# Two output projections of a fused two-block kernel: 256-column products replaced by 512-column products

## The reference

```python
# first block
mixed = jnp.concatenate([o_sb.astype(x.dtype), o_gla], axis=-1) @ w_out[l]
x = x + (1 + gate1[:, None, :]) * mixed
h2 = modulate(rms_norm(x, g_norm2[l]), shift2, scale2)
u = causal_depthwise_conv(h2 @ w_up[l], w_conv[l], b_conv[l])
...
# second block
mix = jnp.concatenate([out_a, out_b], axis=-1) @ w_o[l] + b_o[l]
x = layer_norm(DN_ALPHA * x + mix, ln1_g[l], ln1_b[l])
ca = memory_cross_attention(x, mem, xa_wq[l], ...)
```

## Time and profile before

| | |
|---|---|
| median of three runs | 3327.65 us |
| the profiled execution: its own time | 3335.15 us |
| the profiled execution: its span | 3333.4 us, mean granted clock 0.937 |
| PE busy | 2944.9 us, 88% |
| DVE, ACT, POOL busy | 55%, 31%, 27% |
| out1: first transpose to last early product | 620 to 746 us |
| out2: the same | 2212 to 2335 us |

### The profile page before, as it was taken

How to read it: one execution, slowest core, us unless ns; L and a number is a source line. 1 busy time by engine, 2 the same in 40 slices (tenths; PEclk the granted TensorE clock), 3 DMA queues, 4 the chain that set the end, 5 groups by cost and what they waited for, 6 DMA issues and landing times. The chain is left out here.

```text
span 3333.4 us, 40635 instructions
## 1 busy us (share of the span) xinstructions
PE 2944.9 (88%) x15957; PEld 2528.6 (76%) x15957; DVE 1846.0 (55%) x2924; ACT 1028.8 (31%) x1466; POOL 903.5 (27%) x303
## 2 busy tenths in 40 slices
PE   4969998799999999979577377989999899999996
PEld 3869997688888888868466376779779688888885
DVE  7626775655555454571689676865335533333336
ACT  5414444232221222231556254643221211111111
POOL 1212331112333233240223321221121233333333
PEclk9989998799999999989788678999999999999998
DMA  6732233401101111201323232130101111111111
GB/s 225 269 92 71 71 75 127 162 19 65 51 38 63 38 50 38 76 13 62 97 70 111 60 83 61 43 122 26 57 20 70 64 38 50 50 50 50 50 50 51
DMA packets 112339, 240.06 MB, mean 72 GB/s; under 512 B 53524, under 2 KB 72471, under 8 KB 99015
## 3 DMA queue, kind: packets, MB, share of 16 engines
q1 hardware_dynamic: 107175, 220.70, 20.3%
q10 hardware_dynamic: 4320, 14.29, 1.3%
q0 software_dynamic: 704, 3.15, 0.3%
HBM read 202.58 MB, written 38.67 MB: 72 GB/s over the span
## 5 line engine op out<-in xcount | busy, mean ns | idle before, releaser
L1019 PE MATMUL psum<-h_hi,w_hl 128*128 128x512 f32 x2432 | 751.9, 390 | 16.8 <-DVE ffn_relu L1596 12.8
L1008 POOL TENSOR_TENSOR w_hl<-w_raw,w_hl 128x2048 fp32r<-128x2048 f32 x65 | 323.9, 4983 | 863.5 <-ACT w_hl L1002 863.5
L1019 PEld LDWEIGHTS psum<-h_hi,w_hl 128*128 128x128 f32 x2432 | 457.0, 188 | 113.8 <-issue 18.3
L1036 PE MATMUL psum<-w_hl,ffn_a_hi 128*128 128x512 f32 x1600 | 494.3, 390 | 6.5 <-DVE residual L1359 6.5
L1019 PE MATMUL psum<-h_lo,w_hl 128*128 128x512 f32 x1216 | 474.1, 390 | 0.0
L449 PE MATMUL psum<-w_hl,h_hi 128*128 128x256 f32 (+1 forms) x1920 | 355.8, 288 | 28.4 <-POOL w_hl L412 13.9
L1036 PEld LDWEIGHTS psum<-w_hl,ffn_a_hi 128*128 128x128 f32 x1600 | 301.3, 188 | 69.6 <-DVE residual L1359 6.9
L1002 ACT ACTIVATE w_hl<-w_raw 128x2048 fp32r<-128x2048 f32 x65 | 124.6, 1917 | 692.9 <-PE psum L1036 355.0
L412 POOL TENSOR_TENSOR w_hl<-w_raw,w_hl 128x2048 fp32r<-128x2048 f32 (+1 forms) x39 | 181.3, 4651 | 553.3 <-ACT w_hl L404 553.3
L449 PEld LDWEIGHTS psum<-w_hl,h_hi 128*128 128x128 f32 x1920 | 307.2, 197 | 30.2 <-issue 15.7
L1036 PE MATMUL psum<-w_hl,ffn_a_lo 128*128 128x512 f32 x800 | 311.9, 390 | 0.0
(11 more groups left out here) (347 smaller groups left out, 5066.0 us busy)
## 6 DMA issues: line engine op xcount, KB each, us to landing
w_raw<-in_w_up SPq DMA_DIRECT2D x38, 1024.0 KB, 4.7
w_raw<-in_w_down SPq DMA_DIRECT2D x27, 1024.0 KB, 4.9
ada_w<-in_w_ada ACTq DMA_DIRECT2D x26, 512.0 KB, 4.8
w_raw<-in_w_in_T SPq DMA_DIRECT2D x12, 1024.0 KB, 6.7
ada_w<-in_w_ada SPq DMA_DIRECT2D x22, 512.0 KB, 5.4
w_raw<-in_xa_wkv SPq DMA_DIRECT2D x8, 1024.0 KB, 5.2
w_raw<-in_w_in_G SPq DMA_DIRECT2D x8, 648.0 KB, 5.5
p1G<-sb_stage SPq DMA_DIRECT2D x16, 324.0 KB, 3.7
```

What stands on the lines that cost most here:

```text
L1008: pool.tensor_tensor(self.k.w_lo[s][:, :], self.k.w_raw[s][:, :], self.k.w_hi[s][:, :].bitcast(F), ALU.subtract).then_inc(self.k.wsem["w_r ...
L1019: m = pe.matmul(k.bank[b][:, :], w[:, t * CW + f * P:t * CW + (f + 1) * P], h[:, t, half * 512:half * 512 + 512], start=t == 0 and w is w_ ...
L1036: m = pe.matmul(k.bank[4 + out % 4][:, :], a[f][:, tile * P:(tile + 1) * P], w[:, f * D + half * 512:f * D + half * 512 + 512], start=f == ...
```

## The change

`w_out` and `w_o` become kind "W". Their four chunks are now quarters by row half and column half: chunk 2*ch + half holds rows `half*512` to `half*512+511` of columns `ch*512` to `ch*512+511`, so slot 0 always holds the upper 512 rows and slot 1 the lower. A product has 512 columns; a step of PE (`wide_products`) makes 12 of them for one tile from one slot, and a tile's bank is complete after its second half: 2 column halves x 8 tiles x 2 row halves x 12 = 384 products. Each tile has a bank of its own. Tiles go in two groups of four: all four from slot 0, all four from slot 1, then the next group. `lin_mm` and `lin_evac` are counted by tile. In the second column half the units 0 to 3 stand after tile 7's products from slot 0, units 4 to 7 after tile 5's from slot 1, units 8 to 15 after the last product as before. The source is turned within the steps of the first column half. ACT's program is word for word the same.

```diff
-        self.banks = banks or self.banks
+        self.banks = NT if kind == "W" else banks or self.banks
...
             for name, step in (("w_loaded", 16), ("w_hi_done", 1), ("w_ready", 1), ("lin_mm", self.banks),
-                               ("lin_evac", self.banks)):
+                               ("lin_evac", 0 if kind == "W" and s == self.s0 else self.banks)):
...
+    def wide_products(self, pe, tile, half):
+        k, s, W = self.k, self.s0 ^ half, 2 * CW
+        for t in range(KT // 2):
+            cols, toks = slice(t * W, (t + 1) * W), slice(tile * P, (tile + 1) * P)
+            at = half * KT // 2 + t
+            for w, h in ((k.w_hi[s], self.hh), (k.w_lo[s], self.hh), (k.w_hi[s], self.hl)):
+                mm = pe.matmul(self.wide_bank(tile), h[:, at, toks], w[:, cols],
+                               start=half == 0 and t == 0 and w is k.w_hi[s] and h is self.hh,
+                               stop=half == 1 and t == KT // 2 - 1 and h is self.hl)
+        mm.then_inc(k.wsem["lin_mm"][s], 1)
...
-                        if m == 0:
+                        if wide and m == 0:
+                            pe.wait_ge(*lin.wide_taken(1, 3))
+                        elif wide and KT <= m < KT + 4:
+                            pe.wait_ge(*lin.wide_taken(1, m - KT + 4))
+                        elif m == 0:
...
+                def wide_step(ch, g, half, j):
+                    tile = 4 * g + j
+                    if g == 0 and j == 0:
+                        pe.wait_ge(*lin.at("w_ready", lin.s0 ^ half, ch + 1))
+                    if ch == 0:
+                        if g == 0 and half == 0 and j != 2:
+                            turn_source((0, 1, None, 2)[j])
+                        if g == 0 and (half, j) == (1, 1):
+                            turn_source(3)
+                        pe.wait_ge(src_lo, 2 * tile + half + 1 if g == 0 else 2 * NT)
+                    elif half == 0:
+                        pe.wait_ge(*lin.wide_taken(0, tile))
+                    lin.wide_products(pe, tile, half)
+                    if ch == 1 and g == 1:
+                        if (half, j) == (0, 3):
+                            turn_units(0, 4)
+                        elif (half, j) == (1, 1):
+                            turn_units(4, 4)
+                if wide:
+                    for ch in range(2):
+                        for g in range(2):
+                            for half in range(2):
+                                for j in range(4):
+                                    wide_step(ch, g, half, j)
...
+                def wide_add(ch, tile):
+                    cols = slice(ch * 2 * CW, (ch + 1) * 2 * CW)
+                    dve.wait_ge(*lin.wide_done(ch, tile))
+                    src, xt = lin.wide_bank(tile), k.x[:, tile, cols]
+                    if gate is not None:
+                        dve.tensor_tensor(tmp[:, tile % 2, :], src, gate[:, cols], ALU.mult).then_inc(gated, 1)
+                        dve.wait_ge(gated, NT * ch + tile + 1)
+                        src = tmp[:, tile % 2, :]
+                    dve.tensor_tensor(xt, xt, src, ALU.add).then_inc(k.wsem["lin_evac"][1 ^ lin.s0], 1)
+                    dve.wait_ge(*lin.wide_taken(ch, tile))
+                    dve.bn_stats(st[:, tile, ch, :], xt).then_inc(added, 1)
+                if wide:
+                    for tile in range(NT):
+                        wide_add(0, tile)
+                    dve.wait_ge(gain_in, 16)
+                    dve.wait_ge(shift_in, 16)
+                    for b in range(4):
+                        wide_add(1, 2 * b)
+                        wide_add(1, 2 * b + 1)
+                        pair_norm(b)
+                        if b in (1, 2):
+                            lower(4 * b - 4, 4)
...
+def wide_chunked(w):
+
+    return np.ascontiguousarray(w.reshape(2, KT // 2, P, 2, 2 * CW).transpose(3, 0, 2, 1, 4)).reshape(4, P, KT * CW)
```

More of the change, by code:

```diff
@@ L450, in bank_products, with wide_bank, wide_done, wide_taken @@
         mm.then_inc(k.wsem["lin_mm"][s], 1)
+    def wide_bank(self, tile):
+        return self.k.bank[(4 * self.s0 + tile) % 8]
+    def wide_products(self, pe, tile, half):
[8 more added lines that the diff above has]
+        mm.then_inc(k.wsem["lin_mm"][s], 1)
+    def wide_done(self, ch, tile):
+        return self.at("lin_mm", 1 ^ self.s0, NT * ch + tile + 1)
+    def wide_taken(self, ch, tile):
+        return self.at("lin_evac", 1 ^ self.s0, NT * ch + tile + 1)
     def first_products(self, pe, block_ready):
@@ L695, in residual_norm @@
                   aside_done=None, y_at=None):
-    nc, n = k.nc, lin.n
+    nc, n, wide = k.nc, lin.n, lin.kind == "W"
+    columns_at_once = 2 * CW if wide else CW
     units = [((0, 1, 2, 3), (t,)) for t in range(KT)] + \
@@ L709, in residual_norm @@
         scol = k.sb(c, f"{name}_s", [P, KT])
-        tmp = k.sb(c, f"{name}_gated", [P, 2, CW]) if gate is not None else None
-        st = k.sb(c, f"{name}_st", [P, NT, n, 6])
+        tmp = k.sb(c, f"{name}_gated", [P, 2, columns_at_once]) if gate is not None else None
+        st = k.sb(c, f"{name}_st", [P, NT, D // columns_at_once, 6])
         mv = k.sb(c, f"{name}_mv", [P, NT, 2])
@@ L850, in between @@
                         turn_units(0, 4)
-                lin.products(pe, between, at_source if src is not None else None)
-                turn_units(4, 4)
+                def wide_step(ch, g, half, j):
[22 more added lines that the diff above has]
+                                    wide_step(ch, g, half, j)
+                else:
+                    lin.products(pe, between, at_source if src is not None else None)
+                    turn_units(4, 4)
                 turn_units(8, 4)
@@ L889, in pair_norm @@
                     pair = mv[:, 2 * b:2 * b + 2, :]
-                    dve.wait_ge(added, NT * (n - 1) + 2 * b + 2)
+                    dve.wait_ge(added, NT * (D // columns_at_once - 1) + 2 * b + 2)
                     dve.bn_aggr(mv[:, 2 * b, :], st[:, 2 * b, :, :].rearrange("p c s -> p (c s)")).then_inc(aggr, 1)
@@ L950, in step @@
                             pair_norm(b)
-                lin.chunks(dve, step)
+                def wide_add(ch, tile):
[20 more added lines that the diff above has]
+                            lower(4 * b - 4, 4)
+                else:
+                    lin.chunks(dve, step)
                 lower(8, 8)
@@ L3364, in build @@
                 stick_breaking(k, p1T[0:1024, :], p1V, mix[:, 0:512], lin_G, p1G, mod_stored)
-            lin_out = Linear(k, d["w_out"], D // CW, "N", first_slot=0)
+            lin_out = Linear(k, d["w_out"], D // CW, "W", first_slot=0)
             ffn = Slots(k, (NF1, NF1 // 2), d["w_up"], d["w_down"])
@@ L3402, in build @@
                              d["sinks"], mix[:, 0:512])
-            lin_o = Linear(k, d["w_o"], D // CW, "N", first_slot=0)
+            lin_o = Linear(k, d["w_o"], D // CW, "W", first_slot=0)
             lin_q = Linear(k, d["xa_wq"], D // CW, "T", first_slot=0, halves_first=True)
@@ L3457, in laid_out @@
         "w_in_G": chunked(np.concatenate([gk, gv, gg, gf], 1), GLA_IN // SB_HEADS), "w_fg2": i["w_fg2"][0], "b_fg2": i["b_fg2"][0],
-        "g_gla_out": i["g_gla_out"][0], "w_out": chunked(i["w_out"][0]), "w_up": chunked(up),
+        "g_gla_out": i["g_gla_out"][0], "w_out": wide_chunked(i["w_out"][0]), "w_up": chunked(up),
         "conv": np.ascontiguousarray(conv.transpose(3, 2, 1, 0)), "w_down": row_chunked(i["w_down"][0]),
@@ L3469, in laid_out @@
         "buckets": np.stack([distance_buckets(P), distance_buckets(None)]),
-        "w_o": chunked(i["w_o_2"][0]), "b_o": i["b_o_2"][0], "ln1_g": i["ln1_g_2"][0], "ln1_b": i["ln1_b_2"][0],
+        "w_o": wide_chunked(i["w_o_2"][0]), "b_o": i["b_o_2"][0], "ln1_g": i["ln1_g_2"][0], "ln1_b": i["ln1_b_2"][0],
         "xa_wq": chunked(i["xa_wq_2"][0]), "xa_bq": columns(i["xa_bq_2"][0]), "xa_wkv": chunked(i["xa_wkv_2"][0]),
```

## The result

The changed kernel takes 3357.16 us (median of 5 runs, 3352.76 to 3365.5); the kernel before, run beside it, 3330.17 us (5 runs, 3325.63 to 3334.26). The ratio is 1.009, with a 95% interval of 1.0079 to 1.0102: slower by 26 to 34 us. The medians of e6 and e7 further down each count one far slower run, of 10259.98 and 3548.23 us, which their ratios leave out. The profiled execution has a span of 3354.2 us against 3333.4 before.

The account below looks back on a forecast made before the run. PE, busy 88% of the span, was taken to set the pace in both stages. Out1's +12.4 and out2's +13.7 gave +26.1 us, so the median 3327.65 became about 3353 us, range 3341 to 3364.

Parts of the forecast that it names:

- rival 3: Both stages: gap before unit 10 drops the clock again, start costs its upper bound; +32.7 us, 3360 us, chance 0.12.
- products: Both projections: 384 products of 512 columns at 0.2267 us replace 768 at 0.120 us; gain 5.1 us each.
- start: Start of each stage: PE's first transpose also waits for slot 0's weights; +2.0 us in out1, +3.1 us in out2.
- idle at the end: End of each stage: PE idles waiting for the norm and in the tail; +13.2 us in out1, +13.4 us in out2.
- clock: Behind PE's 12 us idle stretch: some 4.6 us at half speed; +2.3 us in each stage, bounds 0 and 4.6.
- The rival in which the products gain little: Both projections: 512 columns cost twice 256, 0.240 us, so 5.1 us fall away twice; +36.3, 3364 us, chance 0.03.
- 0.6 us more for products at the slow pace: Start of each stage, after the first product: products at the slow pace add 0.6 us.
- E: The end of tile 7's products from slot 0 in the second column half; no ACT root could come before it.
- tiles 2 and 3, each gate and addition at 0.69: Out1's norm before units 0 to 3: with statistics at 0.67, 2 x 2.05 = 4.1 us of the 12.3 us idle.
- The tail: PE's waits at units 8 and 9, 10, 11, and 12 to 15: 0.7 + 3.9 + 1.7 + 0.2 us in out1.
- the norm hides: Before units 0 to 3: roots and scales run under slot 0's four steps; -2.7 us, 3325 us, chance 0.08.
- the stall comes without the clock's fall: Both stages: PE stalls but clock stays or returns at once, start at its lower bound; +17.5, 3345 us, chance 0.15.

Follow-up runs that it names:

- e6: The changed kernel with only the first block's output projection in 512-column products, the second block's as before: 3344.24 us, ratio 1.0051 to the kernel before.
- e7: The changed kernel with ACT's next-matrix cast behind scale(1) and first source transposes ahead of the weights' wait: 3324.54 us, ratio 0.9991 to the kernel before.
- e1: The changed kernel with ACT's cast of the next matrix moved behind scale(1) in the two stages: 3327.63 us, ratio 0.9996 to the kernel before.
- e2: The changed kernel with POOL's subtraction for the next matrix made to wait until tiles 0 to 3 are normed: 3358.07 us (one run).
- e3: The changed kernel with 130 (out1) and 100 (out2) unused transposes on PE ahead of units 0 to 3: 3354.41 us (one run).
- e4: The changed kernel with PE turning the first two source tiles before it waits for slot 0's weights: 3348.44 us (one run).
- e5: The changed kernel with e7's edits plus ACT's emptying of units 4 to 7 ahead of root(2): 3312.03 us, ratio 0.9955 to the kernel before.

## Why the prediction was right, and which terms were off

The forecast, 3353 us and slower, held: the median is 3357.16 us, within the range, and the mechanism is the one named. The size is less well met than the medians suggest. +26.1 us was forecast and the medians differ by 27.0, but the stages show +31.7, which is nearer to rival 3 (+32.7, chance 0.12). The runs' interval, 26 to 34 us, does not separate the two. Point by point, out1 / out2:

| term | forecast, us | measured, us | by |
|---|---|---|---|
| products | -5.1 / -5.1 | -5.1 / -5.1 | pace 0.2267 us, 384 of them |
| start | +2.0 / +3.1 | +2.8 / +3.2 | start of the first product behind 32 transposes, less the 12 products made before it now |
| idle at the end | +13.2 / +13.4 | +15.1 / +12.3 | 20.5 - 5.4 / 15.6 - 3.3 |
| clock | +2.3 / +2.3 | +4.0 / +4.5 | the stage less the other three |
| stage | +12.4 / +13.7 | +16.8 / +14.9 | fixed rows |

**Products.** From 2244.91 to 2306.11 in out2 PE starts 270 products, 0.2267 us each: the pace of the earlier trace rows came over to this stage unchanged. The isolated gap that the Trainium skill gives (TensorE: Matmul & The Clock Gate, Back-to-back issue gap), 215.8 ns by its formula, is 5% below it. The rival in which the products gain little is refuted.

**Start.** The wait for slot 0's weights was as forecast: the transposes began 2.25 and 3.02 us later against the fixed rows than before (forecast 2.2 and 3.0). What was too small in out1 is the "0.6 us more for products at the slow pace": from 622.30 to 625.01 it made six products, 2.71 us, where the full pace would take 1.36, so 1.35 us. That term is partly chance: in the profiles of e1, e2, e3 and e4 out1's products ran at the full pace from the first one on, and the stretch from the first transpose to the first product behind the second 16 took 7.6 to 7.9 us where it took 9.1 in the changed kernel. e4 and e7 showed that the wait is paid in full: 3.1 us less of it in each stage of e4, and stages 3.3 and 2.9 us shorter in e7 than in e1.

**The end.** The mechanism is the one forecast, and e1 proves it: cast, root and the rest in series behind E. In out2 the walk gave 12.2 and the row 11.99. In out1 it gave 12.3 and the row 15.43; the failed step is "tiles 2 and 3, each gate and addition at 0.69", since one of the additions took 4.13 us beside POOL, and e2 showed that without it the gap is 11.99. The tail was forecast at 0.7 + 3.9 + 1.7 + 0.2 and 0 + 3.2 + 1.0 + 0.3, and measured 0.5 + 3.7 + 1.0 + 0 and 0 + 2.9 + 0.7 + 0.

**The clock.** The forecast took one fall a stage and kept a second one for the rival that is worse. The profile has two falls in each stage, and this is the term that was mis-sized. The first cost 1.6 and 2.9 us (e3), close to the 2.3 of the forecast only on average. The second makes it 4.0 and 4.5 us in all, near the bound of 4.6, so that part of the third rival came true. The row that it had the earlier trace rows could not have told: there the clock fell some 4.3 us into the idle stretch, and the gap forecast ahead of unit 10 was 3.9 us. The moment is not fixed by the gap alone: it fell 2.5 us into the gap ahead of unit 10 in out1, 0.7 us into the same gap in e1, and 3.8 us behind its beginning, just after PE had restarted, in e7. What sets it no run here shows.

**The rivals.** That the norm hides is refuted for this kernel and made true by e1, at the place where the prediction put it; the prediction's price for it was -2.7 us. The medians differ by -3.0 us, but the interval of the ratio, 0.9987 to 1.0006, holds no difference, and the stages are only 0.3 and 0.1 us shorter than before: the price left out the second fall of the clock, and the agreement of the medians is luck. That the stall comes without the clock's fall is refuted by the windows.

## What to carry to other kernels

When a buffer is held longer, look for who waits for it ahead of other work in an in-order program: here one cast for the next stage, which takes 1.9 us, held ACT for 30.7 us and VectorE for 13.4 us, and moving it by a few lines was worth 29 us of the median. A reordering of one engine's work must be walked on the other engines too, queue by queue: the last edit, of two calls on ACT, was priced at nothing by looking at TensorE's wait for ACT, and gave 5.1 and 3.9 us through VectorE. And price the half speed behind an idle stretch of TensorE as well as the stretch itself: in these profiles the clock fell with gaps of 3.7 us and of 2.9 us in the tail, and did not with the 2.6 us of the kernel before or the 0.7 to 1.4 us of e5. Last, price a stage from its own rows, and split it before a difference of a microsecond or two is put down to an edit: what the half speed cost behind one and the same wait differed between profiles by up to 1.6 us at the start and 1.4 us behind the first gap.

## What the runs showed of the hardware

An addition on VectorE with both operands in SBUF, 0.69 us alone, took 4.13 us when it was issued 0.9 us behind the start of POOL's subtraction of 128x2048 elements (4.51 us), and ended 0.5 us behind it; in e1, issued at 707.01 while POOL's ran from 703.12 for 4.63 us, it took 1.30 us and again ended 0.6 us behind POOL. Additions and fused operations with one operand in PSUM ran at their usual time beside the same instruction: the addition from PSUM in out2 at 0.67 us. The Trainium skill states this (SBUF — State Buffer, Who interferes with whom): a VectorE instruction with two SBUF inputs and a GpSimd instruction that reads SBUF exclude each other for a whole instruction, and the one issued second waits. The rows agree, and e2 removes the wait by removing the overlap. It cost 3.4 us in the changed kernel, and the prediction had not asked which DVE instructions the moved subtraction would now meet.

What stays open: I did not try whether the remaining waits of e5, 1.16, 0.72 and 1.42 us in the tail of out1, can be closed by another order of units, nor is it shown what makes the rest of the program shorter or longer by some us from one profiled execution to the next, or when the clock falls and rises.
